# A decoder trunk in fp32: the delta rule's blocks kept as compact 64x64 squares

## The reference

```python
a_low = jnp.where(strict, jnp.einsum('bhnid,bhnjd->bhnij', k_beta, k) * decay, 0.0)
t_mat = a_low + jnp.eye(L)                                   # 64x64 per head and chunk
u = triangular_solve(t_mat, v_beta, lower=True, unit_diagonal=True)
w = triangular_solve(t_mat, k_beta * jnp.exp(g)[..., None], lower=True, unit_diagonal=True)
qk = jnp.einsum('bhnid,bhnjd->bhnij', q, k) * decay
...
def step(state, inp):                                        # over the 4 chunks
    v_new = u_i - w_i @ state
    o = q_i @ state + qk_i @ v_new
    state = state * exp(gl_i) + kd_i.T @ v_new
```

## Time and profile before

| | us |
|---|---|
| median of three runs | 2073.72 |
| profiled execution | 2077.49 |
| its span, first to last instruction | 2075.8 |
| TensorE busy in the span | 1953.9 (94%) |
| DVE busy | 1349.7 (65%) |
| ACT busy | 930.5 (45%) |
| POOL busy | 215.0 (10%) |
| delta rule in layer 0, front to last chunk | 332 to 415 |

### The profile page before, as it was taken

How to read it: one execution, slowest core, us unless ns; L and a number is a source line. 1 busy time by engine, 2 the same in 40 slices (tenths; PEclk the granted TensorE clock), 3 DMA queues, 4 the chain that set the end, 5 groups by cost and what they waited for, 6 DMA issues and landing times.

```text
span 2075.8 us, 20939 instructions
## 1 busy us (share of the span) xinstructions
PE 1953.9 (94%) x8341; PEld 1398.0 (67%) x8341; DVE 1349.7 (65%) x1593; ACT 930.5 (45%) x1061; POOL 215.0 (10%) x194
## 2 busy tenths in 40 slices
PE   6999997998899999999889979999999999999996
PEld 5444756745688764475585558878787878787874
DVE  4697267322455449834753138898989898989895
ACT  4231143114444422103511237676767676766664
POOL 7460001100000048100030000000000000000000
PEclk9999998999899999999999979999999999999998
DMA  7334331033655333342300538998989898989891
GB/s 225 122 122 143 141 101 62 1 122 102 201 191 174 126 124 130 122 161 82 122 1 28 184 133 296 337 366 315 370 315 367 314 364 319 364 320 360 322 361 76
DMA packets 202240, 419.53 MB, mean 202 GB/s; under 512 B 8104, under 2 KB 47376, under 8 KB 202144
## 3 DMA queue, kind: packets, MB, share of 16 engines
q1 hardware_dynamic: 196464, 414.20, 55.4%
q0 software_dynamic: 864, 1.69, 0.4%
q10 hardware_dynamic: 4816, 2.34, 0.4%
HBM read 417.17 MB, written 1.05 MB: 201 GB/s over the span
## 4 chain that ended last, share of the span: by engine, by line
PE 84%; DVE 9%; ACT 3%; issue 2%; DMA 1%; ACTq 1%; DVEq 0%
PE bank L1918 22%; PE bank L2314 14%; PE bank L2316 13%; PE bank L2315 13%; PE bank L1911 6%; DVE split_e L1253 3%; PE bank L2411 1%; PE bank L2117 1%; DVE phase L1463 1%; PE bank L2423 1%; PE bank L2182 1%; PE bank L2184 1%; PE bank L1983 1%; PE bank L2440 1%; PE bank L2176 1%
## 5 line engine op out<-in xcount | busy, mean ns | idle before, releaser
L1253 DVE TENSOR_TENSOR split_e<-ring,split_e 128x2048 fp32r<-128x2048 f32 x264 | 600.0, 2289 | 61.6 <-ACT split_e L806 61.6
L806 ACT ACTIVATE split_e<-ring 128x2048 fp32r<-128x2048 f32 x264 | 503.7, 1919 | 185.6 <-PE bank L2316 185.6
L1918 PE MATMUL bank<-ring,hT 128*128 128x512 f32 x768 | 336.6, 596 | 1.7 <-ACT hT L1045 1.7
L2314 PE MATMUL bank<-split_e,fx_e 128*128 128x512 f32 x704 | 282.6, 401 | 2.0 <-DVE fx_e L1775 2.0
L2316 PE MATMUL bank<-split_e,fx_e 128*128 128x512 f32 x704 | 275.0, 391 | 0.0
L2315 PE MATMUL bank<-split_e,fx_e 128*128 128x512 f32 x704 | 274.1, 389 | 0.0
L1918 PEld LDWEIGHTS bank<-ring,hT 128*128 128x128 f32 x768 | 144.2, 190 | 179.2 <-issue 177.1
L2314 PEld LDWEIGHTS bank<-split_e,fx_e 128*128 128x128 f32 x704 | 132.2, 188 | 29.4 <-DVE fx_e L1775 2.2
L2316 PEld LDWEIGHTS bank<-split_e,fx_e 128*128 128x128 f32 x704 | 132.1, 188 | 28.6
L2315 PEld LDWEIGHTS bank<-split_e,fx_e 128*128 128x128 f32 x704 | 132.4, 188 | 27.6 <-issue 1.7
L2314 PE MATMUL bank<-split_e,f_actT_e 128*128 128x512 f32 x352 | 141.5, 402 | 8.4 <-DVE f_actT_e L1783 8.4
(11 more groups left out here) (429 smaller groups left out, 2783.8 us busy)
## 6 DMA issues: line engine op xcount, KB each, us to landing
ring<-in_moe_w_gate SPq DMA_DIRECT2D x40, 2048.0 KB, 9.6
ring<-in_moe_w_up SPq DMA_DIRECT2D x40, 2048.0 KB, 9.5
ring<-in_moe_w_down SPq DMA_DIRECT2D x40, 2048.0 KB, 9.3
ring<-in_w_in SPq DMA_DIRECT2D x28, 2048.0 KB, 7.9
ring<-in_ffn_w_gate SPq DMA_DIRECT2D x11, 1024.0 KB, 5.4
ring<-in_ffn_w_up SPq DMA_DIRECT2D x11, 1024.0 KB, 7.9
ring<-in_ffn_w_down SPq DMA_DIRECT2D x11, 1024.0 KB, 8.7
ring<-in_ssm_w_glu SPq DMA_DIRECT2D x8, 1024.0 KB, 6.1
```

The source lines that it names most:

```text
L806: nc.scalar.activation(split_e[j % NBUF][:, HI, :], ring[:, s * PIECE + i * HGRP:s * PIECE + (i + 1) * HGRP], ACT.Copy).then_inc(split_hi, 1)
L1253: V.tensor_tensor(split_e[j % NBUF][:, LO, :], ring[:, s * PIECE + i * HGRP:s * PIECE + (i + 1) * HGRP], split_e[j % NBUF][:, HI, :].bitca ...
L1918: last = mm(B[bank][:, :], src[:, k, t * P:(t + 1) * P], w[:, k, n0:n0 + 512], start=k == 0, stop=k == kt - 1)
L2314: mm(bank, a[HI], w[HI], start=first, stop=False)
```

## The change

All matrices of a chunk are stored as 64x64 squares, both chunks of a tile on their own 64 partitions: a tile's four heads take 256 columns in place of 512. X and Z lie side by side in one tensor `XZ`. What changes by step:

- The front's decay tensors `dec` and `decT` have half the columns; `kds` goes and `kdec` reads its factor from `decT`. The k.k and k.q products are computed per head and chunk into one bank each, behind both `kv_evac`; `A_low` takes two operations and `qkT` one, for both tiles together.
- POOL writes `XZ` with two copies in place of four, then waits once for `A_low` and cuts out all six levels in a row, into six `M_lvl` tensors.
- The level's products are made per head and block, 64 rows by 64 columns, blocks 0 and 1 in turn, in banks 2t+b (W) and 4+2t+b (X and Z in one bank). ACT and DVE handle each block's 64 partitions with their own instruction.
- u is no longer formed and copied. w^T is copied with the factor -1, and each chunk's `vn` is summed in PSUM from Z^T vbeta and (from chunk 1) -w times state; DVE only copies it. Chunk 0 leaves the state out of `vn`, of the output and of the state update.
- At the start POOL builds the masks at full width and adds their halves into `level_mask`, `ident2` and `causal2`.

The diff, cut to its core; most removed lines are left out, since they stand in the listing above, and the indentation is shortened:

```diff
...
+dec_buf, decT_buf, qkT_buf = rg.take(NT, GH, P), rg.take(NT, GH, P), rg.take(NT, GH, P)
+
+def compact(v):
+    return v.rearrange("p (t h n) -> p t h n", t=NT, h=GH)
+
+def flat(v):
+    return v.rearrange("p t h n -> p (t h n)")
+
+HB = NT * GH * GL
+dec, decT, qkT = (compact(flat(v)[:, 0:HB]) for v in (dec_buf, decT_buf, qkT_buf))
 vn = rg.take(GH, GD)
...
+wT = dec_buf
 o_tok, g_oT = k_tok, kbeg.rearrange("p t h d -> p (t h d)").rearrange("p (k n) -> p k n", k=KW)
...
+XZ = uT[:, :, :].rearrange("p q n -> p (q n)").rearrange("p (t a h n) -> p t a h n", t=NT, a=2, h=GH)
 state = v_tok[:, :, :].rearrange("p t (h n) -> p t h n", h=GH)
...
+rq = [kbeg, vbeta, kdec, qkT_buf]
+halves = [spare_half(i // 2, i % 2) for i in range(6)]
+A_low, W_lvl, DTm, Dcl = (compact(halves[i][:, j * HB:(j + 1) * HB]) for i in (0, 3) for j in range(2))
+M_lvl = [compact(halves[(1, 2, 4)[k // 2]][:, (k % 2) * HB:(k % 2 + 1) * HB]) for k in range(6)]
+gdiag = compact(halves[5])
...
     for k in range(6):
         b = 2 ** k
...
+        q = wide[:, k, :].rearrange("p (a h b) -> p a h b", h=2, b=b)[:, :, 0, :]
         link(nc.gpsimd.memset(q, 1.0))
         keep(q, [[-2 * b, P // (2 * b)], [0, b]], -b, 1)
         keep(q, [[2 * b, P // (2 * b)], [0, b]], 2 * b - 1, -1)
+    link(nc.gpsimd.tensor_tensor(level_mask[:, :, :], wide[:, :, 0:GL], wide[:, :, GL:P], ALU.add))
+    link(nc.gpsimd.tensor_tensor(ident2[:, :], ident[:, 0:GL], ident[:, GL:P], ALU.add))
+    link(nc.gpsimd.tensor_tensor(causal2[:, :], cum_mask[:, 0:GL], cum_mask[:, GL:P], ALU.add))
     link(nc.gpsimd.memset(causal[:, :], 0.0))
     for at in (0, 2 * P):
...
         for t in range(NT):
...
+            nc.gpsimd.tensor_copy(XZ[:, t].rearrange("p a h n -> p (a h) n"),
+                                  ident2[:, :].unsqueeze(1).to_broadcast([P, 2 * GH, GL])).then_inc(xz_init, 1)
+        pool.wait_ge(a_ready, l + 1)
         for k in range(6):
             for t in range(NT):
...
+                nc.gpsimd.tensor_tensor(M_lvl[k][:, t], A_low[:, t],
+                                        level_mask[:, k, :].unsqueeze(1).to_broadcast([P, GH, GL]),
                                         ALU.mult).then_inc(m_ready, 1)
...
@@ -1019,12 +1027,18 @@
             for t in range(NT):
                 n = (6 * l + k) * NT + t
                 act.wait_ge(w_ps, n + 1)
...
+                for b in range(2):
+                    r_ = slice(b * GL, (b + 1) * GL)
+                    last = nc.scalar.activation(W_lvl[r_, t], B[2 * t + b][r_, 0:GH * GL].rearrange("p (h n) -> p h n", h=GH),
+                                                ACT.Copy)
+                last.then_inc(w_evac, 1)
         for t in range(NT):
             act.wait_ge(uw_ps, NT * l + t + 1)
...
+            for b in range(2):
+                last = nc.scalar.activation(wT[:, t, :, b * GL:(b + 1) * GL],
+                                            B[2 * t + b][:, 0:GH * GL].rearrange("p (h n) -> p h n", h=GH),
+                                            ACT.Copy, scale=-1.0)
+            last.then_inc(w_done, 1)
...
             dve.wait_ge(row_ps, NT * l + t + 1)
...
+            for b in range(2):
+                r_ = slice(b * GL, (b + 1) * GL)
+                last = V.tensor_tensor(DTm[r_, t], B[2 + t][r_, :].rearrange("p (h n) -> p h n", h=GH)[:, :, r_],
+                                       gc3[r_, t, :].unsqueeze(2).to_broadcast([GL, GH, GL]), ALU.subtract)
+            link(last)
...
             dve.wait_ge(dec_ready, 3 * NT * l + 3 * t + 3)
...
+            link(V.tensor_tensor(decT[:, t], decT[:, t], causal2[:, :].unsqueeze(1).to_broadcast([P, GH, GL]),
                                  ALU.mult))
...
         def per_token(s3, t):
...
             V.tensor_tensor(kbeg[:, t], k_tok[:, t], per_token(bx3, t), ALU.mult)
...
+            V.tensor_tensor(kdec[:, t], k_tok[:, t], decT[:, t, :, GL - 1].unsqueeze(2).to_broadcast([P, GH, GD]),
+                            ALU.mult)
             dve.wait_ge(kv_ps, 4 * l + 2 + t + 1)
             V.scalar_tensor_tensor(vbeta[:, t], B[6 + t][:, :].rearrange("p (h n) -> p h n", h=GH), 0.5,
                                    per_token(be3, t), ALU.mult, ALU.mult).then_inc(uw_in, 1)
+        be2 = beta.unsqueeze(2).to_broadcast([P, NT * GH, GL])
+
+        def heads(v):
+            return v.rearrange("p t h n -> p (t h) n")
+
+        dve.wait_ge(kk_ps, 2 * l + 1)
+        link(V.tensor_tensor(heads(A_low), B[4][:, :].rearrange("p (h n) -> p h n", n=GL), heads(dec), ALU.mult))
+        V.tensor_tensor(heads(A_low), heads(A_low), be2, ALU.mult).then_inc(a_ready, 1)
+        dve.wait_ge(kk_ps, 2 * l + 2)
+        V.tensor_tensor(heads(qkT), B[5][:, :].rearrange("p (h n) -> p h n", n=GL), heads(decT), ALU.mult).then_inc(qk_ready, 1)
         for t in range(NT):
...
             qc = cv[:, 0:4, t * P:(t + 1) * P]
             V.tensor_tensor(qc, qc, e_row[:, t], ALU.mult).then_inc(qd_ready, 1)
...
+                    dve.wait_ge(xz_init, NT * l + t + 1)
                 dve.wait_ge(xz_ps, n + 1)
...
+                for b in range(2):
+                    r_ = slice(b * GL, (b + 1) * GL)
+                    v = XZ[r_, t].rearrange("p a h n -> p (a h n)")
+                    last = V.tensor_tensor(v, v, B[4 + 2 * t + b][r_, :], ALU.subtract)
+                last.then_inc(xz_ready, 1)
             for t in range(NT):
                 dve.wait_ge(xz_ready, (6 * l + k) * NT + t + 1)
...
         for c in range(NCHUNK):
             n, t, off = NCHUNK * l + c, c // 2, (c % 2) * GL
             rows_ = slice(off, off + GL)
             dve.wait_ge(vn_ps, n + 1)
...
+            V.tensor_copy(vn[rows_], B[c % 2][rows_, :].rearrange("p (h n) -> p h n", h=GH)).then_inc(vn_ready, 1)
             if c < NCHUNK - 1:
                 new, old = state[:, (c + 1) % 2], state[:, c % 2]
...
+                if c > 0:
+                    eg = e_row[:, t, :, off + GL - 1].unsqueeze(2).to_broadcast([P, GH, GD])
+                    dve.wait_ge(s_ready, n - l)
+                    link(V.tensor_tensor(new, old, eg, ALU.mult))
                 dve.wait_ge(su_ps, (NCHUNK - 1) * l + c + 1)
...
+                su = B[7][:, :].rearrange("p (h n) -> p h n", h=GH)
+                (V.tensor_tensor(new, new, su, ALU.add) if c > 0 else V.tensor_copy(new, su)).then_inc(s_ready, 1)
         dve.wait_ge(o_evac, NCHUNK * (l + 1))
         o_all = o_tok.rearrange("p t h n -> p (t h) n")
...
+        pe.wait_ge(kv_evac, NT * (l + 1))
+        for a, bank in ((4, 4), (0, 5)):
+            for t in range(NT):
+                for h in range(GH):
+                    for b in range(2):
+                        at, j = slice(t * P + b * GL, t * P + (b + 1) * GL), t * GH + h
+                        last = mm(B[bank][b * GL:(b + 1) * GL, j * GL:(j + 1) * GL], cv[:, 4 + h, at], cv[:, a + h, at],
+                                  start=True, stop=True)
             last.then_inc(kk_ps, 1)
...
+
+        blocks = [(h, b, slice(b * GL, (b + 1) * GL)) for h in range(GH) for b in range(2)]
         for k in range(6):
             for t in range(NT):
                 n = (6 * l + k) * NT + t
                 pe.wait_ge(m_ready, n + 1)
                 if k == 0:
...
+                    pe.wait_ge(xz_init, NT * l + t + 1)
                     pe.wait_ge(dec_in, NT * (l + 1))
                     pe.wait_ge(dec_ready, 3 * NT * (l + 1))
                     pe.wait_ge(xk_sb, 6 * l + 2)
                 else:
                     pe.wait_ge(xz_ready, n - NT + 1)
...
+                for h, b, r_ in blocks:
+                    last = mm(B[2 * t + b][r_, h * GL:(h + 1) * GL], M_lvl[k][r_, t, h, :], XZ[r_, t, 1, h, :],
+                              start=True, stop=True)
                 last.then_inc(w_ps, 1)
             for t in range(NT):
                 n = (6 * l + k) * NT + t
+                if k == 0:
+                    pe.wait_ge(qk_ready, l + 1)
+                    pe.wait_ge(uw_in, NT * (l + 1))
                 pe.wait_ge(w_evac, n + 1)
...
+                for h, b, r_ in blocks:
+                    mm(B[4 + 2 * t + b][r_, h * GL:(h + 1) * GL], W_lvl[r_, t, h, :], XZ[r_, t, 0, h, :],
+                       start=True, stop=True)
+                for h, b, r_ in blocks:
+                    last = mm(B[4 + 2 * t + b][r_, (GH + h) * GL:(GH + h + 1) * GL], XZ[r_, t, 0, h, :], W_lvl[r_, t, h, :],
+                              start=True, stop=True)
                 last.then_inc(xz_ps, 1)
         for t in range(NT):
             pe.wait_ge(xz_ready, (6 * l + 5) * NT + t + 1)
...
+            for h, b, r_ in blocks:
+                last = mm(B[2 * t + b][:, h * GL:(h + 1) * GL], kbeg[r_, t, h, :], XZ[r_, t, 1, h, :], start=True, stop=True)
             last.then_inc(uw_ps, 1)
         pe.wait_ge(w_done, NT * (l + 1))
...
+        pe.wait_ge(qd_ready, NT * (l + 1))
         arrived(l, U_WV)
         for c in range(NCHUNK):
             n, t, off = NCHUNK * l + c, c // 2, (c % 2) * GL
```

(29 more changed lines are left out.)

91 lines of the change are left out of this document (9 added, 82 removed).

## The result

The median of the changed kernel is 2099.34 us (2096.33 to 2099.74, 4 runs) against 2077.91 us of the kernel before beside it: ratio 1.0101 [1.0068, 1.0134]. Forecast: 2056, faster. The profiled execution has a span of 2097.7 us, 21.9 more than before.

The account below looks back on a forecast made before the run. TensorE was taken to bound the inversion and chunk loop, DVE the stretch just before. Gains 3.5 + 7.9 + 1.1 - 3.7 = 8.8 us a layer, 17.6 for two, took the profiled 2077.49 to 2059.9, median 2056; range 2046 to 2077.

Parts of the forecast that it names:

- Chunk loop: Chunk loop: alternating tile sizes lengthen vn in chunks 1 to 3; net loss 3.7 us a layer, bounds 0 to 5.6.
- Front: Before the inversion levels: halved ACT and DVE work, fewer operations; gain 3.5 us a layer, bounds -0.9 to +3.9.
- Levels: Inversion levels: small neighbouring tiles overlap; 26.8 us including 1.5 for a slow-clock start, gain 7.9 a layer.
- Period: Time per inversion level, set by a ring of TensorE products and DVE subtractions: 4.6 us, bounds 4.1 to 10.7.
- Rival 1: Inversion levels: TensorE's issue or non-overlapping tiles hold a pair at 0.055 us or more; total 2074, chance 0.20.
- Rival 3: Inversion levels: price per instruction does not fall with size, pairs stay at 0.111 us; total 2120, chance 0.07.
- End of the inversion: After the levels: fewer products, u copy gone; 2.1 us for 3.2, gain 1.1 a layer, 0.2 without tile overlap.
- Start: Kernel start: POOL builds compact masks in about 1.7 us, covered by its idle time; cost 0, or 1.7 uncovered.
- Rival 2: Inversion levels: clock stays at 1.2 GHz, chunk loop's first products cost 1.5 more a layer; total 2073, chance 0.09.
- Rival 4: Chunk loss hidden or POOL's masks never bind, gain near the level ring's floor of 4.1 us; total 2045, chance 0.04.
- slower: Whole kernel: outcome of a measured time over 2084.1 us, given chance 0.10.

Follow-up runs that it names:

- experiment 2: Kernel before, full-array levels, with only the new vn sum in PSUM (no u, chunk 0 without the state): 2081.57 us, ratio 1.0020.
- experiment 3: Changed kernel plus three unused full-array products of 512 columns between the w products and the chunk loop: 2059.59 us, ratio 0.9922.
- experiment 4: Changed kernel plus u's products issued behind those for w into free banks, result unused: 2060.52 us, ratio 0.9906.
- experiment 8: Changed kernel with the two products of odd heads in turned order, in vn and in the output: 2094.75 us, ratio 1.0087.
- experiment 9: Changed kernel with the first product of each vn sum on 128-row key tiles and all of vbeta (other values): 2057.16 us, ratio 0.9919.
- experiment 10: Kernel before with new vn sum and six extra ACT copies ahead of each loop, first product on 128-row keys: 2092.55 us, ratio 1.0073.
- experiment 11: Kernel before with new vn sum and six extra ACT copies ahead of each loop, both sum products on 64*64 tiles: 2120.08 us, ratio 1.0215.
- experiment 1: Changed kernel with the old end of the inversion and old chunk loop put back, on compact blocks: 2057.09 us, ratio 0.9902.
- experiment 13: Changed kernel's compact levels, u copied as before, zero state left out of chunk 0, output order turned in odd heads: 2053.45 us, ratio 0.9892.
- experiment 14: Compact levels with old end and chunk loop, full chunk 0, only the output order turned in odd heads: 2047.51 us, ratio 0.9863.
- experiment 5: Changed kernel with POOL's building of the masks moved behind its first transfers and fills: 2097.35 us, ratio 1.0108.
- experiment 7: Kernel before with the new vn sum in PSUM and six extra chained ACT copies delaying TensorE ahead of each chunk loop: 2133.47 us, ratio 1.0259.

## Why the prediction was wrong

The step that failed is "Chunk loop": -3.7 a layer, bounds 0 and 5.6. It priced every product of the loop at 2.4 GHz. From its first vn product to the start of the remaining memory values the loop took 427.91 - 382.92 = 45.0 us, against 414.74 - 391.67 = 23.1 before: +21.9. At 2.4 GHz it is +2.9 (26.0 us in experiments 2, 3 and 4), within the bounds and 0.8 less than the sum had: the sum's first 64*64 products start beside the last ones of the output (403.29 and 403.30 in experiment 4) and slide under them. The other 19.0 is the clock, for which the term had no place. The memory values behind the loop, still at 1.2 GHz to 431.4, add 1.7 (the changed kernel is 13.2 us behind the kernel before at their start and 14.9 at their end). In layer 1 the loop took 43.6 us, 17.6 of them the clock's.

- *Front.* Forecast 3.5; the first subtraction is at 353.50 (353.77 before) although DVE arrived 3.5 late at the front: 3.7. (The parts of the forecast add up to 3.7 too; the sum took 3.5.) In part this is luck. DVE reached kbeg at 342.52, only 0.7 earlier than before when the 3.5 is taken off, not 1.5; in return the k-k products cost 0.1, and the stretch of DVE behind A_low, counted as equal, came out some 0.6 smaller (L1570 1.97 for two, L1574 1.75, L1576 1.63). POOL's twelve products took 11.10 us and not 8: eight of them 0.72 each, near the 0.67 forecast, but the four beside L1570, L1574 and L1576 1.17 to 1.71.
- *Levels.* 353.50 to 381.00 is 27.5 us, forecast 26.8; gain 7.2 for 7.9. Period 4.70 for 4.6; the slow start, at a granted clock of 0.72 from 348 to 360, made the first period 5.91, so 1.2 for the 1.5 put aside. Rivals 1 and 3, on the price of a pair, were refuted.
- *End of the inversion.* 1.92 us, forecast 2.1; gain 1.3 for 1.1. But it is this shorter end that lets the clock fall (experiments 3 and 4): the worth of a removed product was taken as its time alone.
- *Start.* Forecast 0. This execution was 3.0 late at 40 us and 3.5 from 50 on, with TensorE at 1.2 GHz for 17.1 us ahead of 52.5; another with the same start (experiment 8) had 10.2 us and was 0.3 and 1.4 early. POOL's 1.75 us are real; the rest varies.
- *Rival 2* had the right mechanism in the wrong place. It asked whether the levels would stay cold, priced the chunk loop by its "first products" alone (1.5 a layer), and so gave 2073 and a chance of 0.09. In the levels TensorE was busy 13.92 of 19.60 us at a clock of 1.00. The prediction never asked whether a loop with 64-row tiles in its sum gets the clock back, and the trace before could not show it: its loop never fell.
- The upper end of 2077 covered rivals 1 and 2 as they were priced. Rivals 1, 3 and 4 and the forecast itself let the chunk loop run at 2.4 GHz throughout, and the 0.10 for "slower" came from other causes.

Two rules of the Trainium skill. The rule weighed ahead ("TensorE: Matmul & The Clock Gate", section "Wait — 56ns, not 53.3ns?"), 62 ns per MATMUL with hardware decode off, does not bind here: 0.029 us. The same section gives a floor of about 25 ns between starts, however small the product; I had overlooked it. The trace's mean of 0.029 agrees, though single starts stand 0.022 apart, and the first two of a group 0.007. Its section "Loop structure matters more than you think" says that back-to-back matmuls keep the array warm; here 47.80 us of 47.80 busy stood at 0.50, so the measurement decides: with 64*64 tiles in the sum, back-to-back was not enough to get it back.

Open: each kernel's stretches are those of one profiled execution, though the medians go with them. Experiments 9 to 11 change the numbers in the operands along with their rows (the inverse is triangular, so that near half of a 64*64 tile is zeros; the keys are not), and no run keeps them apart. All loops, the old one too, have other 64-row products, in the output and the state update, so the runs show no share at which it tips. What exactly lets the clock fall at the end of the inversion is known by examples alone, and busy time does not sort them. In the 8 us ahead of the loop TensorE was busy 5.59 us in the changed kernel, which fell, 6.74 and 7.19 with u's products or the filler, which held, and 5.80 in 1, 13 and 14, of which only 13 fell, behind its loop's start.

## What to carry to other kernels

Read the granted clock by stretches before and after each place where an edit thins out TensorE's work, and price a fall by how long the work behind it takes to get back: here 10 to 14 us with 128*64 tiles in the sum, 7 to 24 in loops without a second product in it, and the whole loop with 64*64 ones. Work taken out just ahead of a stage of small tiles can cost many times its own length, and dead work put there can pay (2.8 us of filler a layer gained some 40 in all). Put products of equal tile size next to each other: 0.14 us a switch.

## What the runs showed of the hardware

- A busy TensorE stayed at 1.2 GHz for 37 to 51 us, until the end of the loop, in all ten falls with 64*64 tiles in the sum (experiments 5, 7, 8, 11 and the changed kernel); it came back in 10.2 to 13.7 us once the sum was 128*64 alone (9, 10).
- At 1.2 GHz two instructions of alternating size take 0.62 us, eight of one size 1.97 with the tail (1.06 to 1.08 at 2.4 GHz).
- A two-input product of 256 columns on POOL takes 0.72 us, and 1.17 to 1.71 in the four that ran beside DVE's L1570, L1574 and L1576; one of 512 columns, in the kernel before, takes 1.27, and up to 1.72 beside DVE.
